# ScalarE reads the recurrence's sums straight from PSUM in a two-layer transformer kernel

## What is computed

```python
log_w = -jnp.exp(-jax.nn.softplus(-(w0 + jnp.tanh(w_lo) @ w_up)) - 0.5)   # = -exp(-0.5) * sigmoid(w0 + ...)
a = jax.nn.sigmoid(a0 + a_lo @ a_up)
g = jax.nn.sigmoid(g_lo) @ g_up
kk = kk * lax.rsqrt(jnp.sum(kk * kk, axis=-1, keepdims=True) + 1e-12)
k = k * (1.0 + (a - 1.0) * k_a)
_, y = lax.scan(step, s0, seq)          # the recurrence, here in four chunks of 64 tokens
y = ((y - ym) * lax.rsqrt(yv + RWKV_GN_EPS)).reshape(B, S, RWKV_W) * gn_g + gn_b
return ((y + bonus) * g).astype(p.dtype)
```

## Time and profile before

| | us |
|---|---|
| median of 3 runs | 2428.0 (2420.35 to 2428.21) |
| the profiled execution | 2439.14 |
| its span, first to last instruction | 2437.4 |
| PE busy in it | 2329.9 (96%) |
| DVE busy | 1603.8 (66%) |
| ACT busy | 1155.4 (47%) |
| mean granted TensorE clock | 0.977 of full |

### The profile page before, as it was taken

How to read it: one execution, slowest core, us unless ns; L and a number is a source line. 1 busy time by engine, 2 the same in 40 slices (tenths; PEclk the granted TensorE clock), 3 DMA queues, 4 the chain that set the end, 5 groups by cost and what they waited for, 6 DMA issues and landing times.

```text
span 2437.4 us, 43524 instructions
## 1 busy us (share of the span) xinstructions
PE 2329.9 (96%) x16455; PEld 1988.8 (82%) x16455; DVE 1603.8 (66%) x3556; ACT 1155.4 (47%) x2149; POOL 0.2 (0%) x4
## 2 busy tenths in 40 slices
PE   7998999999989999999999899999999999999998
PEld 3864788888884799998888899997888899778885
DVE  4568565555477777766576876857667755659893
ACT  3237354444335665644213655543403644458881
POOL 0000000000000000000000000000000000000000
PEclk8998999999999999999899999999899999999999
DMA  9237559998325679746456498545553765469996
GB/s 360 90 103 271 170 180 372 373 373 315 95 87 175 206 244 334 246 132 199 159 180 225 136 334 304 156 135 182 182 166 130 277 207 182 147 224 344 337 356 240
DMA packets 256239, 544.25 MB, mean 223 GB/s; under 512 B 28448, under 2 KB 28704, under 8 KB 255520
## 3 DMA queue, kind: packets, MB, share of 16 engines
q1 hardware_dynamic: 256032, 541.48, 65.0%
HBM read 473.21 MB, written 68.16 MB: 222 GB/s over the span
## 4 chain that ended last, share of the span: by engine, by line
PE 84%; DVE 12%; issue 2%; ACT 2%; DMA 0%; SPq 0%; DVEq 0%; ACTq 0%
PE bank L967 11%; PE bank L971 11%; PE bank L970 11%; PE bank L1330 4%; PE bank L929 4%; PE bank L1333 4%; PE bank L1334 4%; PE bank L1297 3%; PE bank L1217 2%; PE bank L987 2%; PE bank L1300 2%; PE bank L1301 2%; PE bank L991 2%; PE bank L990 2%; PE bank L1265 2%
## 5 line engine op out<-in xcount | busy, mean ns | idle before, releaser
L2761 DVE TENSOR_TENSOR WL<-ring,WH 128x512 fp32r<-128x512 f32 x632 | 417.1, 686 | 183.5 <-ACT WH L1934 181.7
L1934 ACT ACTIVATE WH<-ring 128x512 fp32r<-128x512 f32 x632 | 380.2, 624 | 271.8 <-PE bank L967 182.8
L2854 DVE TENSOR_TENSOR WLE<-slots,WHE 128x1024 fp32r<-128x1024 f32 x231 | 281.4, 1224 | 116.3 <-ACT WHE L1934 111.9
L1934 ACT ACTIVATE WHE<-slots 128x1024 fp32r<-128x1024 f32 x231 | 244.7, 1061 | 115.4 <-PE bank L1330 74.5
L967 PE MATMUL bank<-AH,WH 128*128 128x256 f32 (+1 forms) x832 | 266.0, 320 | 10.8 <-DVE AL L2559 4.4
L971 PE MATMUL bank<-AH,WL 128*128 128x256 f32 (+1 forms) x832 | 264.7, 318 | 0.0
L970 PE MATMUL bank<-AL,WH 128*128 128x256 f32 (+1 forms) x832 | 264.6, 318 | 0.0
L967 PEld LDWEIGHTS bank<-AH,WH 128*128 128x128 f32 x832 | 158.5, 190 | 24.0 <-DVE AL L2559 4.9
L970 PEld LDWEIGHTS bank<-AL,WH 128*128 128x128 f32 x832 | 157.6, 189 | 11.1
L971 PEld LDWEIGHTS bank<-AH,WL 128*128 128x128 f32 x832 | 157.5, 189 | 11.2
L967 PE MATMUL bank<-HH,WH 128*128 128x256 f32 (+1 forms) x528 | 166.5, 315 | 0.0
(11 more groups left out here) (449 smaller groups left out, 5762.8 us busy)
## 6 DMA issues: line engine op xcount, KB each, us to landing
ring<-stream SPq DMA_DIRECT2D x864, 256.0 KB, 4.4
slots<-experts SPq DMA_DIRECT2D x264, 512.0 KB, 5.2
WH<-gate_high_parts SPq DMA_DIRECT2D x128, 256.0 KB, 2.8
WL<-gate_low_parts SPq DMA_DIRECT2D x128, 256.0 KB, 3.6
SQ<-stream SPq DMA_DIRECT2D x86, 256.0 KB, 4.7
gate_high_parts<-SQ SPq DMA_DIRECT2D x86, 256.0 KB, 3.9
gate_low_parts<-SQ SPq DMA_DIRECT2D x86, 256.0 KB, 4.4
S<-stream SPq DMA_DIRECT2D x42, 256.0 KB, 4.6
```

What stands on the lines that cost most here:

```text
L1934: return nc.scalar.activation(o, i, fn, **kw)
L2761: V.tensor_tensor(WL[:, s % SPLIT, :], ring[:, c % RING, :], WH[:, s % SPLIT, :].bitcast(F32), ALU.subtract).then_inc(w_taken, 1)
L2854: V.tensor_tensor(WLE[:, s % PAIR_SPLIT, :], pair(pair_of(s)), WHE[:, s % PAIR_SPLIT, :].bitcast(F32), ALU.subtract).then_inc(pair_taken, 1)
```

## The change

The seven sums of the head are no longer copied out by VectorE. ScalarE takes the root of unit k and the sigmoids of units k+1 to k+4 straight from PSUM, with the added constant as a bias column, and copies `GV` out of units k+5 and k+6. The factor -exp(-0.5) moves from a VectorE operation to the scale of the three exponentials. ScalarE's two gate tiles that stood ahead of the root now stand behind it, ahead of the sigmoids. VectorE gives the units back after ScalarE has read them (`given_back(n)`, a one-element memset that raises `gemm_free` by n): unit k once the root is there, units k+1 to k+6 in one step behind the operation of line 3392. In the tail the copy of `YC` into `YT` is dropped (the two names change places), and ScalarE takes the root of the variance from PSUM with 1/64 as scale.

```diff
@@ -68,7 +68,7 @@
     ("ada_b0", 48), ("ada_b1", 48), ("n1g0", KD), ("n1g1", KD), ("n2g0", KD), ("n2g1", KD), ("final_g", KD),
-    ("sgu_b", 512), ("lqk", 256), ("subln", 1), ("odd_sink", 16), ("sgu_w", 512), ("router_w", 64), ("router_b", 8), ("spare", 13), ("eps5_scaled", 1),
+    ("sgu_b", 512), ("lqk", 256), ("subln", 1), ("odd_sink", 16), ("sgu_w", 512), ("router_w", 64), ("router_b", 8), ("eps12", 1), ("spare", 12), ("eps5_scaled", 1),
 ]
@@ -784,6 +784,10 @@
+        def halves_of(b):
+
+            return b[:, :].rearrange("p (a b) -> p a b", a=2)
+
         def rows_of(c):
@@ -1908,7 +1912,7 @@
                 ready_wait()
-                dup_unit(cn("blk64"), YT[:, :, :].rearrange("p a b -> p (a b)"), 512)
+                dup_unit(cn("blk64"), YC[:, :, :].rearrange("p a b -> p (a b)"), 512)
                 gates(TAIL_GATES[1])
@@ -2377,22 +2381,32 @@
                 gates(l, 1)
-                act.wait_ge(rw_asked, 5 * l + 1)
+                act.wait_ge(rw_asked, 2 * l + 1)
                 f(LOW[0:64, 0, :], RP[0:64, 6, :], ACT.Tanh)
                 f(LOW[:, 1, :], RP[:, 7, :], ACT.Sigmoid).then_inc(rw_low, 1)
+                u = UB[l]["knorm"]
+                act.wait_ge(gemm_done, u + 1)
+                f(KNORM, halves_of(bank[u % BANKS]), ACT.Sqrt, bias=pr("eps12")).then_inc(rw_given, 1)
                 gates(l, 2)
-                act.wait_ge(rw_asked, 5 * l + 2)
-                f(KNORM, KNORM, ACT.Sqrt).then_inc(rw_given, 1)
-                act.wait_ge(rw_asked, 5 * l + 3)
-                f(LWV, LWV, ACT.Sigmoid)
-                f(AV, AV, ACT.Sigmoid).then_inc(rw_given, 1)
-                act.wait_ge(rw_asked, 5 * l + 4)
-                f(EC, CC, ACT.Exp)
-                f(EN, CC, ACT.Exp, scale=-1.0)
-                f(EX, EX, ACT.Exp).then_inc(rw_given, 1)
+                for n, (o, by) in enumerate(((LWV, f"w0_{l}"), (AV, f"a0_{l}"))):
+                    for j in range(2):
+                        v = u + 1 + 2 * n + j
+                        act.wait_ge(gemm_done, v + 1)
+                        ins = f(o[:, j, :], bank[v % BANKS][:, 0:T], ACT.Sigmoid, bias=pr(by, j, j + 1))
+                ins.then_inc(rw_given, 1)
+                for j in range(2):
+                    act.wait_ge(gemm_done, u + 5 + j + 1)
+                    ins = f(GV[:, j, :], bank[(u + 5 + j) % BANKS][:, 0:T], ACT.Copy)
+                ins.then_inc(rw_given, 1)
+                act.wait_ge(rw_asked, 2 * l + 2)
+                decay = float(np.exp(-0.5))
+                f(EC, CC, ACT.Exp, scale=-decay)
+                f(EN, CC, ACT.Exp, scale=decay)
+                f(EX, EX, ACT.Exp, scale=-decay).then_inc(rw_given, 1)
                 gates(l, 1 + 2 + 2 + 5 + 3)
-                act.wait_ge(rw_asked, 5 * l + 5)
-                f(YS, YS, ACT.Sqrt, bias=pr("epsgn")).then_inc(rw_given, 1)
+                u = UB[l]["merge"] - 1
+                act.wait_ge(gemm_done, u + 1)
+                f(YS, halves_of(bank[u % BANKS]), ACT.Sqrt, bias=pr("epsgn"), scale=1.0 / HD).then_inc(rw_given, 1)
                 gates(l, 2 + 1)
@@ -2423,7 +2437,7 @@
             V = nc.vector
-            st = dict(u=0, a=0, g=0, tmp=0, chain=0, c=0, h=0, p=0, pair=0)
+            st = dict(u=0, a=0, g=0, tmp=0, chain=0, c=0, h=0, p=0, pair=0, back=0)
@@ -2461,6 +2475,12 @@
                 mark(ready)
+
+            def given_back(n):
+
+                V.memset(small(285 + st["back"], 1), 0.0).then_inc(gemm_free, n)
+                st["u"] += n
+                st["back"] += 1
@@ -3357,31 +3377,19 @@
                 link(ins)
-                mark(rw_asked, 5 * l + 0)
+                mark(rw_asked, 2 * l)
                 for j in range(2):
...
                 branches(l, 2)
-                b = take()
-                kn = KNORM[:, :, :].rearrange("p a b -> p (a b)")
-                free(V.tensor_scalar(kn, b[:, :], 1e-12, None, ALU.add))
-                settled()
-                mark(rw_asked, 5 * l + 1)
-                for j in range(2):
-                    free(V.tensor_scalar(LWV[:, j, :], take()[:, 0:T], pr(f"w0_{l}", j, j + 1), None, ALU.add))
-                for j in range(2):
-                    free(V.tensor_scalar(AV[:, j, :], take()[:, 0:T], pr(f"a0_{l}", j, j + 1), None, ALU.add))
-                settled()
-                mark(rw_asked, 5 * l + 2)
-                copy_units([GV[:, j, :] for j in range(2)])
-                dve.wait_ge(rw_given, 4 * l + 1)
+                assert st["u"] == UB[l]["knorm"]
+                dve.wait_ge(rw_given, 5 * l + 1)
+                given_back(1)
                 link(V.reciprocal(KNORM, KNORM))
                 link(V.tensor_tensor(KK, KK, KNORM, ALU.mult))
-                dve.wait_ge(rw_given, 4 * l + 2)
-
-                link(V.tensor_scalar(LWV, LWV, -float(np.exp(-0.5)), None, ALU.mult))
+                dve.wait_ge(rw_given, 5 * l + 2)
                 for j in range(2):
@@ -3390,9 +3398,11 @@
                 link(V.scalar_tensor_tensor(RP[:, 2:4, :], BON, 1.0, RP[:, 2:4, :], ALU.add, ALU.mult))
+                dve.wait_ge(rw_given, 5 * l + 3)
+                given_back(6)
                 branches(l, 2)
                 link(V.tensor_tensor(BH, KK, AV, ALU.mult))
-                dve.wait_ge(rw_given, 4 * l + 3)
+                dve.wait_ge(rw_given, 5 * l + 4)
                 V.tensor_tensor(KR[:, :, 0, :], KK, EX, ALU.mult)
@@ -3470,20 +3480,16 @@
-                link(V.tensor_copy(YT, YC))
                 go()
                 b = take()[:, :].rearrange("p (a b) -> p a b", a=2)
-                link(V.scalar_tensor_tensor(YC, b, -1.0 / HD, YT, ALU.mult, ALU.add))
-                free(V.tensor_tensor(YS, YC, YC, ALU.mult))
+                link(V.scalar_tensor_tensor(YT, b, -1.0 / HD, YC, ALU.mult, ALU.add))
+                free(V.tensor_tensor(YS, YT, YT, ALU.mult))
                 settled()
                 go()
-                b = take()[:, :].rearrange("p (a b) -> p a b", a=2)
-                free(V.tensor_scalar(YS, b, 1.0 / HD, None, ALU.mult))
-                settled()
-                mark(rw_asked, 5 * l + 4)
-                dve.wait_ge(rw_given, 4 * l + 4)
+                dve.wait_ge(rw_given, 5 * l + 5)
                 link(V.reciprocal(YS, YS))
-                link(V.tensor_tensor(YC, YC, YS, ALU.mult))
+                given_back(1)
+                link(V.tensor_tensor(YC, YT, YS, ALU.mult))
                 for j in range(2):
@@ -3542,7 +3548,7 @@
         u += 23 + 6 + 4
-        out[l] = {"index": u}
+        out[l] = {"index": u, "knorm": u + 8 + 10}
         u += 8 + len(PAIRS) - KD
@@ -3861,6 +3867,7 @@
     put("eps6", 1e-6)
+    put("eps12", 1e-12)
     put("eps5", 1e-5)
```

## The result

The changed kernel takes 2442.2 us (median of 7 runs, 2434.3 to 2451.9), the kernel before beside it 2428.2 us (7 runs). The ratio of the runs is 1.0045 with a 95% interval of 1.0023 to 1.0066: slower by 0.45%, 5.6 to 16 us (the two medians alone lie 14.0 us apart). That the median falls on the forecast to a tenth is chance; runs of one kernel scatter by 10 us and more. The sum behind it is read better from the profile.

A forecast was written before the change was run, and what follows sets the result against it. TensorE was taken to bound the kernel. Per layer 8.0 - 1.8 - 0.7 + 1.8 - 0.2 = 7.1 us, 14.2 us for two layers on a median of 2428.0, gave 2442.2 us; 8 in 10: 2434 to 2450 us.

The forecast's parts named there:

- The bound: TensorE holds 84% of the span; only its waits in head and tail, 3.2 us a layer, can be won back.
- The stall: Head, ahead of the branch products: TensorE newly waits for units given back late, 8.0 us a layer.
- What the stall gives back ahead of the transposes: Head: TensorE's waits of 1.42 us (gate tile) and 0.39 us (transposes) vanish, minus 1.8 us a layer.
- The clock: Behind the new gap in the head TensorE's clock falls to half, plus 1.8 us a layer, between 0 and 3.3.
- The bank waits behind the transposes: Head: TensorE's waits of 0.16 and 0.55 us for banks vanish, minus 0.7 us a layer.
- The tail: Wait of 0.71 us ahead of the last branch products goes, mostly returning in the output projection; minus 0.2 us a layer.
- a stall at its bare length: Rival, head: clock back within a microsecond and one table load, 4.4 us a layer, 2436.8 us; chance 0.15.
- a clock that stays down: Rival, head: half clock through most of the 12.4 us behind the stall, 10.3 us a layer, 2448.6 us; chance 0.13.
- the faster one: Rival, head: units come back in time, all five waits go, up to 3.2 us a layer, 2421.5 us; chance 0.05.

The follow-up runs named there:

- Run 1: Changed kernel, but VectorE gives units k+1 to k+4 back right after the four sigmoids, ahead of the scan; ratio to the kernel before 1.0013.
- run 2: Changed kernel, but each ScalarE instruction that reads one of the seven units raises gemm_free itself; ratio to the kernel before 1.0013.
- run 6: Against run 2, the two gate tiles moved behind the sigmoids and the GV copies; ratio to the kernel before 0.9994.
- run 5: Changed kernel with 13 unread fp32 matmuls in a gate bank ahead of the head's branch products; ratio to the kernel before 1.0051.
- run 3: Kernel before with only the tail's part of the change; ratio to the kernel before 0.9997.
- runs 6 and 7: run 6, and a kernel made from run 6 with sigmoids first and sums of squares, root and reciprocal last; the latter's ratio to the kernel before 0.9978.
- run 8: Kernel before with only the head's root taken from PSUM, ahead of the gate tiles, VectorE's other copies kept; ratio to the kernel before 1.0017.
- fill of 26: Changed kernel with 26 unread fp32 matmuls in a gate bank ahead of the head's branch products; ratio to the kernel before 1.0076.

## Why the prediction was right, point by point

**The bound** was read rightly: of all the work taken off VectorE, only TensorE's waits came back, and the one new wait decided.

**The stall** was forecast at 8.0 us between 7.1 and 8.3, and is 7.74. The reciprocal starts 2.47 us behind unit k's matmul (forecast 2.55), the scan 7.57 us (7.55). The sigmoids do need a table load of their own: three loads stand between the root and the exponentials. I had written that the trace before doesn't show this. It has two rows, ahead of the earlier trace rows, that bear on it:

```profile
1215.87 0.42 ACT L1934 ACTIVATE S<-S 64x256 f32<-64x256 f32 x1 [6.27 <-DVE smalls L2459]
1216.29 1.28 ACT L1934 ACT_TABLE_LOAD   x1
```

The tanh of `LOW` is followed by a load ahead of the sigmoid of `LOW`, so there a table was in use that served tanh and was not kept for the sigmoid, while none stands between the sigmoid and the tiles' tanh behind it. Order counts, and the changed kernel puts tanh first. Run 1 and run 2 show that the place of `given_back(6)` sets the stall and not ScalarE's list, run 6 that the tiles and their extra load were 2.1 us of the path to the first sigmoid. The rule of the Trainium skill that I had weighed (ScalarE activation tables: per-element evaluation and per-set limits, section Table sets in the compiler and the runtime) would have had one load serve tiles and sigmoids. The trace disagrees: a load for the tiles, another for the sigmoids 0.84 us of work later.

**What the stall gives back ahead of the transposes** was put at 1.8 us, the two listed waits (1.81), and these are gone. With the listed numbers 7.74 - 1.81 + 1.89 is the 7.82 us by which the stretch to the transposes grew, but to the hundredth that is chance. The starts of the rows show the parts better; these two are from the kernel before:

```profile
1225.11 1.89 PE L929 MATMUL bank<-A,ring 128*128 128x256 f32 x8
1241.29 1.89 PE L929 MATMUL bank<-A,ring 128*128 128x256 f32 x8
```

| us, layer 0 | before | after | difference |
|---|---|---|---|
| unit k's matmul to the first branch products | 2.98 | 11.05 | +8.07 |
| these to the next branch products | 4.58 | 6.56 | +1.98 |
| these to the transposes | 9.61 | 7.38 | -2.23 |
| transposes to the branch products behind them | 6.57 | 5.17 | -1.40 |
| these to the output projection | 84.37 | 84.11 | -0.26 |

Two listed waits of 1.81 us together cost 2.23 us of starts, and the stall of 7.74 us delays the branch products by 8.07 us, 0.17 of it because unit k+6 comes later (the row of the six units takes 2.37 us, not 2.20; I had allowed 0.1). So each of these stops cost some 0.2 us more than the idle time that the profile lists.

**The clock** was put at 1.8 us a layer between 0 and 3.3. It is 1.89 by the branch matmuls and 1.9 by run 5. The fall is as forecast, but that the size fits so well is in part luck: I reckoned with 3.3 us at half clock behind the stall, and there were 6.8 us, 3 of them while TensorE was idle. Run 2's two layers, 2.88 and 3.78 us behind equal waits, show how this term moves with the moment of the fall.

**The bank waits behind the transposes** were under-sized. I subtracted the two listed waits, 0.7 us, and 1.4 us came back (the fourth row of the table). The small matmuls behind the transposes (96 records) run in one row of 2.44 us after, where before they are two rows, of 1.10 and 1.89 us, with a wait ahead of each; there is also a stop of under 0.1 us near 1239.65, too short to be listed. Again the stops cost more than their listed idle time.

**The tail** was put at -0.2 us and is -0.27 (run 3), with the gain turned into a longer wait where I had said.

The sum is thus 6.16 us in layer 0 instead of 7.1, 12.2 us for both instead of 14.2; 0.7 us of the 0.94 that are missing is the bank term. That the timings admit 14.2 us too says nothing for that term. **Of the chances**, 0.68 for slower by over 0.5% was somewhat high for a sum so near that line: one timing puts it at 0.45%, the other at 0.58%. The rivals of a stall at its bare length and of a clock that stays down didn't happen. The second was priced too low: 12.4 us of work at 7 instead of 11 matmuls a microsecond take 7.1 us more, not 4.5, which makes it 12.4 us a layer and 2453 us, beyond the range of 8 in 10. Nor did the faster one happen, though runs 6 and 7 show that it was a matter of order and of one counter.

## What to carry to other kernels

When an operation that reads a PSUM bank moves to another engine, ask first when the bank is given back and by whom, and what TensorE has queued for that bank; a reader that finishes early helps nobody if the engine that signals for it is deep in its own chain. Let the reader itself raise the counter (7.74 us of stall became 3.24 in run 2), and compute the units in the order in which they can be released. Among ScalarE's operations, put those of one table next to each other, above all where TensorE waits for the first behind the load (3.24 us became 1.09 in run 6). And read every layer's stretch: layer 0 alone shows run 2 as 0.9 us better than run 1, and in layer 1 that gain is gone.

## What was not expected of the hardware

In run 8, waits of TensorE of 1.80 us (layer 0) and 1.79 us (layer 1) for a gate tile were each followed by a clock at half, 0.9 and 1.4 us after they ended; the waits of 1.42 us there in the kernel before were not. But the length of a wait alone doesn't decide it. Behind a wait of 1.81 us in the output projection of layer 0 the clock stayed full in the kernel before and fell in run 8. And in work that the change doesn't touch, a wait of 3.60 us left the clock at half in the kernel before (0.50 from 193 to 196) and full in the changed one (1.00 from 187 to 200); the same four records then took 1.11 us and 0.66 us:

```profile
193.00 1.11 PE L1250 MATMUL bank<-con,S 128*128 128x128 f32 x4 [3.60 <-DVE S L2690]
```

```profile
192.17 0.66 PE L1254 MATMUL bank<-con,S 128*128 128x128 f32 x4 [3.60 <-DVE S L2710]
```

What decides it no run here shows, so a gap of such a length can be given only a range of cost. In the fill of 26, TensorE's clock stayed full on matmuls with unread results. And an fp32 matmul of 256 columns stands in the profile as two records of 0.22 us each, 0.44 us in all (11.49 us for 26).
